# A two-block transformer step on one core: small operations of the linear-attention solve go to ScalarE, its end is written in a new order, and key products stand among the pair products

## The reference, cut to what matters

```python
def _rwkv7_step(S, inp):
    r, w, k, v, a, b = inp
    sa = jnp.einsum('bhvk,bhk->bhv', S, a)
    S = S * w[:, :, None, :] + sa[..., None] * b[:, :, None, :] + v[..., None] * k[:, :, None, :]
    y = jnp.einsum('bhvk,bhk->bhv', S, r)
    return S, y

    S0 = jnp.zeros((B, H, N, N), f32)
    _, y = lax.scan(_rwkv7_step, S0, seq)
    mean = jnp.mean(y, axis=-1, keepdims=True)
    var = jnp.mean(jnp.square(y - mean), axis=-1, keepdims=True)
    yn = ((y - mean) * lax.rsqrt(var + LNX_EPS)).reshape(B, T, D) * lnx_w + lnx_b
    bonus = (jnp.sum(rh * kh * r_k, axis=-1, keepdims=True) * vh).reshape(B, T, D)
    out = ((yn + bonus) * g).astype(x.dtype)
    return out @ w_o
...
    x = x + rmsnorm(m, norm_g[layer, 1])
    f = conv_ffn(rmsnorm(x, norm_g[layer, 2]), ffn_w_in[layer], ...)
```

## Time and profile before

| | us |
|---|---|
| median of 3 runs | 1098.86 |
| lowest and highest of the 3 | 1093.63, 1102.5 |
| the profiled execution, its own time | 1091.18 |
| the profiled execution, its span on the core | 1089.3 |
| PE busy in the span | 1062.2 (98%) |
| DVE, ACT, POOL busy | 798.9, 604.0, 219.3 |
| the stretch that the change touches, from the second pair products to the first feed-forward tile | 122 to 219 |

### The profile page before, as it was taken

How to read it: one execution, slowest core, us unless ns; L and a number is a source line. 1 busy time by engine, 2 the same in 40 slices (tenths; PEclk the granted TensorE clock), 3 DMA queues, 4 the chain that set the end, 5 groups by cost and what they waited for, 6 DMA issues and landing times.

```text
span 1089.3 us, 18693 instructions
## 1 busy us (share of the span) xinstructions
PE 1062.2 (98%) x7143; PEld 917.0 (84%) x7143; DVE 798.9 (73%) x1103; ACT 604.0 (55%) x928; POOL 219.3 (20%) x234
## 2 busy tenths in 40 slices
PE   7999998999999999999999999999999999999997
PEld 6997797888888888789888888998777789888886
DVE  7997878778886658777788756688867776666643
ACT  6766363555564566856666554635665446555532
POOL 0125493121221011002222200571100001122200
PEclk9999999999999999999999999999999999999999
DMA  8553172646666466345667575556452555766552
GB/s 249 172 172 117 39 244 69 175 135 181 187 192 253 167 151 162 121 131 150 187 189 192 194 271 158 159 191 215 154 136 84 194 162 131 193 191 193 193 193 78
DMA packets 219747, 183.11 MB, mean 168 GB/s; under 512 B 43265, under 2 KB 197614, under 8 KB 219678
## 3 DMA queue, kind: packets, MB, share of 16 engines
q1 hardware_dynamic: 215710, 171.43, 52.4%
q0 software_dynamic: 3392, 8.66, 2.5%
q10 hardware_dynamic: 576, 2.07, 0.5%
HBM read 179.44 MB, written 2.69 MB: 167 GB/s over the span
## 4 chain that ended last, share of the span: by engine, by line
PE 80%; DVE 13%; issue 2%; DMA 2%; ACT 1%; POOL 1%; SPq 1%; DVEq 0%; POOLq 0%; ACTq 0%
PE bank L288 20%; PE bank L282 13%; PE bank L284 13%; PE bank L283 13%; PE bank L289 10%; DVE ring L417 3%; PE bank L295 2%; PE bank L1250 2%; DVE arena L1687 1%; DVE arena L1782 1%; DVE stat L1780 1%; PE bank L375 1%; PE bank L2167 1%; DMA arena<-in_kv_w_up 1%; PE bank L1365 1%
## 5 line engine op out<-in xcount | busy, mean ns | idle before, releaser
L417 DVE TENSOR_TENSOR ring<-ring,arena 128x2048 fp32r<-128x2048 f32 (+1 forms) x138 | 312.9, 2271 | 112.4 <-ACT arena L411 110.8
L282 PE MATMUL bank<-arena 128*128 128x512 f32 (+3 forms) x980 | 343.6, 351 | 3.7 <-DVE ring L417 3.0
L288 PE MATMUL bank<-arena 128*128 128x512 f32 x960 | 335.7, 396 | 0.0
L411 ACT ACTIVATE arena<-ring 128x2048 fp32r<-128x2048 f32 (+1 forms) x145 | 272.1, 1879 | 98.0 <-DMA ring<-in_ffn_w_out 42.9
L289 PE MATMUL bank<-arena,ring 128*128 128x256 f32 x960 | 267.2, 278 | 0.0
L284 PE MATMUL bank<-arena 128*128 128x512 f32 (+3 forms) x720 | 264.7, 368 | 0.0
L283 PE MATMUL bank<-ring,arena 128*128 128x512 f32 (+2 forms) x560 | 216.1, 386 | 0.0
L288 PEld LDWEIGHTS bank<-arena 128*128 128x128 f32 x960 | 180.1, 188 | 42.6
L282 PEld LDWEIGHTS bank<-arena 128*128 128x128 f32 x980 | 185.4, 189 | 29.2 <-issue 5.4
L289 PEld LDWEIGHTS bank<-arena,ring 128*128 128x128 f32 x960 | 180.6, 188 | 0.0
L284 PEld LDWEIGHTS bank<-arena 128*128 128x128 f32 x720 | 135.6, 188 | 22.2
(11 more groups left out here) (338 smaller groups left out, 1274.9 us busy)
## 6 DMA issues: line engine op xcount, KB each, us to landing
ring<-in_ffn_w_in SPq DMA_DIRECT2D x80, 512.0 KB, 5.1
ring<-in_ffn_w_out SPq DMA_DIRECT2D x44, 512.0 KB, 4.4
ring<-in_w_gate_up SPq DMA_DIRECT2D x40, 512.0 KB, 5.1
ring<-in_w_in SPq DMA_DIRECT2D x18, 1024.0 KB, 5.1
ring<-in_a_w_rkv SPq DMA_DIRECT2D x12, 1024.0 KB, 5.4
ring<-in_w_down SPq DMA_DIRECT2D x22, 512.0 KB, 3.7
ring<-in_a_w_o SPq DMA_DIRECT2D x4, 1024.0 KB, 6.8
arena<-in_ffn_w_in SPq DMA_DIRECT2D x8, 512.0 KB, 4.7
```

The costliest lines, as they stand in the source:

```text
L282: nc.tensor.matmul(dst, stationary[0], moving[0], start=start, stop=False)
L288: nc.tensor.matmul(dst[:, :], stationary[0], both_parts, start=start, stop=False)
L411: nc.scalar.activation(buf(hi_of(n), 0, w, arena12), ring[:, r, 0:w], ACT.Copy).then_inc(hi_ready, 1)
L417: on.tensor_tensor(ring12[:, r, 0:w], ring[:, r, 0:w], buf(hi_of(n), 0, w, arena12).bitcast(F32), ALU.subtract).then_inc(split_ready, 1)
```

## The change

It has these parts:

1. **Key products among pair products.** On PE `key_values(0)` stands behind bank 9 and `key_values(1)` behind bank 12 of the second pass, instead of both behind bank 15.
2. **Means of the values.** DVE sums both chunks in one reduction and no longer scales; ACT scales (`v_mean`), before its first `step_evac`. POOL's `values_centred` waits for that.
3. **Variance.** DVE keeps the reduction (`squares_summed`); ACT does the scaling (`variance`).
4. **Scaling of the outputs.** The multiplication of a bank by the root moves from one DVE operation to eight ACT operations, one for each head (`scaled`), so `gated_out` has two DVE operations left.
5. **Order on DVE.** The first sum of squares stands ahead of `state_added`; both `gated_out` of chunk 0 stand behind the last `block_added`; the last `w_o` split stands ahead of `gated_out(1, 0)`; `early_lo(0)` leaves the solve for the passage, and `early_lo(1)` goes behind the first turn there.
6. **Order on PE.** `block_inverses(1, 1)` stands ahead of `o_turn(0, 0)`; `o_turn(1, 1)` stands ahead of tile (1, 0), not (1, 1).
7. **Order on ACT.** The squares of chunk 1 stand closer together, and the second `w_o` slot's high part is split once the state products are done.
8. **POOL** waits for the low part of the first `w_o` slot before `values_centred(1)`.

Two semaphores are renamed: `means_ready` is `stats_ready` (it counts the sums too), `u_out` is `solve_out` (it counts `scaled` too, so `EARLY_OUT0` is 8).

```diff
@@ ffn_front_dve
             if f != 1:
+                early_lo(dve, f, 0 if f == 0 else 1)
+            turn_dve(dve, turn, 0, 4, hi, lo)
+            if f == 0:
                 early_lo(dve, f, 1)
-            turn_dve(dve, turn, 0, 4, hi, lo)
@@ rwkv_pe
             pe.wait_ge(tok_evac, 4)
-            for l in range(PAIR_BANKS):
-                if l >= 4:
-                    pe.wait_ge(prod_evac, PAIR_BANKS + l - 3)
-                pairs(l, key, l // 8).then_inc(prod_mm, 1)
...
-            pe.wait_ge(v_evac, 4)
-            key_values(0)
-            key_values(1)
+            for l in range(PAIR_BANKS):
+                if l >= 4:
+                    pe.wait_ge(prod_evac, PAIR_BANKS + l - 3)
+                pairs(l, key, l // 8).then_inc(prod_mm, 1)
+                if l == 9:
+                    pe.wait_ge(v_evac, 4)
+                    key_values(0)
+                elif l == 12:
+                    key_values(1)
             pe.wait_ge(z_landed, 16 * NT * NB)
             pe.wait_ge(cleared, NT * NB + 1)
             pe.wait_ge(prod_evac, 2 * PAIR_BANKS)
...
             block_inverses(1, 0)
+            block_inverses(1, 1)
             o_turn(0, 0)
-            block_inverses(1, 1)
...
                 elif (a, s) == (1, 0):
+                    o_turn(1, 1)
                     pe.wait_ge(o_split, 3)
-                elif (a, s) == (1, 1):
-                    o_turn(1, 1)
@@ rwkv_act
             def squares(a, q):
                 act.wait_ge(ymm, 2 * a + q + 1)
-                if a == 1:
-                    act.wait_ge(var_ready, 2 + q + 1)
...
+            def variance(a, q):
+                stat = slice(a * H + 8 * q, a * H + 8 * (q + 1))
+                act.wait_ge(stats_ready, 2 + 2 * a + q + 1)
+                nc.scalar.activation(y_var[:, stat], y_sq[:, stat], ACT.Copy, bias=LNX_EPS, scale=1.0 / N).then_inc(var_ready, 1)
+
+            def scaled(a, q):
+                act.wait_ge(rstd_ready, 2 + 2 * a + q + 1)
+                for h in range(8 * q, 8 * q + 8):
+                    op = nc.scalar.activation(toks(W_YC)[:, a, h * N:(h + 1) * N], bank[Y_BANK[a][q]][:, h % 8 * N:(h % 8 + 1) * N],
+                                              ACT.Copy, scale=y_rstd[:, a * H + h:a * H + h + 1])
+                op.then_inc(solve_out, 1)
...
+            act.wait_ge(stats_ready, 1)
+            nc.scalar.activation(v_mean, v_sum, ACT.Copy, scale=-1.0 / N).then_inc(stats_ready, 1)
             for b in range(4):
                 step_evac(b)
...
             squares(0, 0)
+            act.wait_ge(state_mm, 1)
+            ahead(act, FIRST["w_o"] + 1, split_act)
+            variance(0, 0)
             squares(0, 1)
+            variance(0, 1)
             ahead(act, FIRST["w_o"] + 2, split_act)
+            scaled(0, 0)
+            scaled(0, 1)
             act.wait_ge(sweep_mm, SOLVED + SWEEP_NO[1, 2])
             ahead(act, LAST["w_o"], split_act)
             solutions(1, 0)
             solutions(1, 1)
             o_evac(0, 0)
             squares(1, 0)
+            squares(1, 1)
             o_evac(0, 1)
-            squares(1, 1)
+            variance(1, 0)
+            variance(1, 1)
             early_hi(act, 0, 0)
+            scaled(1, 0)
+            scaled(1, 1)
@@ rwkv_dve, gated_out
-                dve.wait_ge(rstd_ready, 2 + 2 * a + q + 1)
-                link(dve, nc.vector.tensor_tensor(by_head(yc), by_head(bank[Y_BANK[a][q]][:, :]), spread(y_rstd[:, stat].unsqueeze(2), [P, 8, N]), ALU.mult))
+                dve.wait_ge(solve_out, 4 * a + 2 + q + 1)
@@ rwkv_dve
-            for a in range(NT):
-                value_means(a)
+            nc.vector.tensor_reduce(v_sum, by_head(buf(W_V)), AX, ALU.add).then_inc(stats_ready, 1)
...
+            squares_summed(0, 0)
             state_added(0)
             state_added(1)
-            variance(0, 0)
+            squares_summed(0, 1)
             block_added(1, 0, 1)
-            variance(0, 1)
             block_added(1, 0, 2)
             block_added(1, 1, 1)
-            gated_out(0, 0)
             block_added(1, 0, 3)
             block_added(1, 1, 2)
             block_added(1, 1, 3)
+            gated_out(0, 0)
             gated_out(0, 1)
             o_lo(0, 0)
             ahead(dve, FIRST["w_o"] + 1, split_dve)
-            variance(1, 0)
+            squares_summed(1, 0)
             o_lo(0, 1)
-            variance(1, 1)
+            squares_summed(1, 1)
             ahead(dve, FIRST["w_o"] + 2, split_dve)
+            ahead(dve, LAST["w_o"], split_dve)
             gated_out(1, 0)
-            ahead(dve, LAST["w_o"], split_dve)
             gated_out(1, 1)
             o_lo(1, 0)
-            early_lo(dve, 0, 0)
             o_lo(1, 1)
@@ rwkv_pool
-                pool.wait_ge(means_ready, a + 1)
+                pool.wait_ge(stats_ready, 2)
...
             rest_gated(0)
+            pool.wait_ge(split_ready, SPLIT_NO[FIRST["w_o"]] + 1)
             values_centred(1)
```

More of the change, by code:

```diff
@@ L1448, in rwkv_pe @@
                 if h % 8 == 0:
-                    pe.wait_ge(u_out, h // 8 + 1)
+                    pe.wait_ge(solve_out, h // 8 + 1)
                 lo, c, hv = (h % 2) * N, h // 2, slice(h * N, (h + 1) * N)
@@ L1476, in rwkv_pe @@
             block_inverses(1, 0)
+            block_inverses(1, 1)
             o_turn(0, 0)
[L1478 removed]
             for q in range(2):
[L1480 removed]
+                pe.wait_ge(solve_out, 4 + q + 1)
                 y_solved(1, q)
@@ L1638, in solutions @@
                 act.wait_ge(sweep_mm, SOLVED * a + SWEEP_NO[g, NB])
-                nc.scalar.activation(u[a][:, g * HALF:(g + 1) * HALF], bank[(0, 4)[a] + g][:, :], ACT.Copy).then_inc(u_out, 1)
+                nc.scalar.activation(u[a][:, g * HALF:(g + 1) * HALF], bank[(0, 4)[a] + g][:, :], ACT.Copy).then_inc(solve_out, 1)
             def squares(a, q):
                 act.wait_ge(ymm, 2 * a + q + 1)
-                if a == 1:
-                    act.wait_ge(var_ready, 2 + q + 1)
                 nc.scalar.activation(y_squared[q], bank[Y_BANK[a][q]][:, :], ACT.Square).then_inc(squared, 1)
+            def variance(a, q):
[8 more added lines that the diff above has]
+                op.then_inc(solve_out, 1)
             def o_evac(a, q):
@@ L1799, in at_bank, with squares_summed @@
                 return toks(W_YC)[:, a, q * HALF:(q + 1) * HALF], slice(a * H + 8 * q, a * H + 8 * (q + 1))
-            def variance(a, q):
+            def squares_summed(a, q):
                 stat = at_bank(a, q)[1]
                 dve.wait_ge(squared, 2 + 2 * a + q + 1)
-                link(dve, nc.vector.tensor_reduce(y_sq[:, stat], by_head(y_squared[q]), AX, ALU.add))
-                nc.vector.tensor_scalar(y_var[:, stat], y_sq[:, stat], 1.0 / N, LNX_EPS, ALU.mult, ALU.add).then_inc(var_ready, 1)
+                nc.vector.tensor_reduce(y_sq[:, stat], by_head(y_squared[q]), AX, ALU.add).then_inc(stats_ready, 1)
             def gated_out(a, q):
@@ L1836, in block_added @@
                 nc.vector.tensor_tensor(rhs[a][rows, cells], bank[g][rows, :], rhs[a][rows, cells], ALU.add).then_inc(sum_ready, 1)
-            def value_means(a):
-                at = slice(a * H, (a + 1) * H)
-                link(dve, nc.vector.tensor_reduce(v_sum[:, at], by_head(toks(W_V)[:, a, :]), AX, ALU.add))
-                nc.vector.tensor_scalar(v_mean[:, at], v_sum[:, at], -1.0 / N, None, ALU.mult).then_inc(means_ready, 1)
             def state_added(g):
```

11 lines of the change are left out of this document (5 added, 6 removed).

## The result

The changed kernel takes 1087.03 us (median of 4 runs, 1085.12 to 1091.76) against 1100.3 for the kernel before in the same comparison (median of 4, which include the three shown above). The ratio is 0.9893, with a 95% interval of [0.9862, 0.9923]. Repeated with more runs, it was 1087.99 (8 runs), ratio 0.9904 [0.9876, 0.9932]. The prediction had summed up 0.5 us.

A forecast was written before the change was run, and what follows sets the result against it. PE, busy in 98% of the span, was taken as the bound; time is won only where DVE, ACT or POOL end its waits last. The terms left 0.5 us at the passage; forecast 1097 us, range 1091 to 1102.

The forecast's parts named there:

- Part 2: Means of the values: the blocked 1.18 us scaling leaves DVE, POOL's first centring starts near 139.7 or later, nothing on PE.
- the signs of being right: Trace signs listed beforehand, from steps starting 1 to 2 us later than 136.47 to the clock at 0.50 near 128.
- Part 1: Keys among pair banks: +0.85 exposed copy, -0.3 filled waits, +0.6 lone banks; steps about 1.2 us later.
- the lone banks: Pair banks 12 and 15, left without a partner by the moved keys: 0.6 us taken, bounds zero and 2 x 0.5.
- Parts 3 to 5: Chunk 1's sweep: PE's 2.1 us of addition waits go, but ACT's chain leaves the w_o tiles' start unchanged (-1.5 to +1).
- ACT takes over: In chunk 1's sweep: sixteen ACT scalings end at 171.6, the solutions at 174.8, losing 2 us of the sweep's gain.
- The w_o tiles: Output tiles paced by DVE's 11.0 us chain: gate at 186.7, tile (0, 3) at 187.2 against 187.10, so zero gain.
- Part 8 and the state: POOL's wait holds DVE's first w_o low part to 154.5, ending near 156.8; the state 0.4 us late.
- The passage: Solve to feed-forward: post_scale near 191.6, chunk 0's turn wait vanishes, x_scaled ends at 204.2 against 204.70; 0.5 us left.
- The front costs nothing and ACT keeps up: Rival: state 1.2 us early, sweep saves 2.1 more; -3 us in the median, 1094 to 1096; chance 0.17.
- The front costs more than the tail returns: Rival: steps 2 us later, POOL and DVE collide at the low part; +0.3 to +2, 1099 to 1101; chance 0.22.
- The scalings bind: Rival: an ACT scaling out of PSUM takes 0.35, not 0.25 us; 1.6 before chunk 1's solutions, +1.5; chance 0.06.

The follow-up runs named there:

- the means alone: Kernel before with only one reduction of both chunks on DVE and the scaling on ACT: 1092.11 us (12 runs), ratio 0.9959.
- the POOL wait: Kernel before with one line more, POOL waiting for both means before chunk 1's read mask: 1091.44 us (12 runs), ratio 0.9948.
- second trace of before: Kernel before, unchanged, run again for another trace: 1099.4 us (10 runs), ratio 0.9998; the trace's span is 1095.2 us.
- keys and means back: Changed kernel with both key halves behind the last pair bank and the means scaled on DVE again: 1094.51 us (12 runs), ratio 0.9928.
- the passage alone: Kernel before with only o_turn(1, 1) one tile earlier and the new places of early_lo: 1095.4 us (12 runs), ratio 0.9948.
- means back: Changed kernel with the means' two reductions and two scalings on DVE again: 1088.58 us (11 runs), ratio 0.9926.
- keys alone: Kernel before with only the key products moved among the pair products: 1095.31 us (12 runs), ratio 0.9965.
- the passage back: Changed kernel with the last output turn and both early low parts placed as before: 1089.07 us (12 runs), ratio 0.9925.

## Why the prediction was wrong

**The step that failed** stands in "What bounds the kernel now", in "Nothing that I found reaches 1% (11 us) in either direction", and in Part 2, which ends "nothing on PE" and priced only "the blocked 1.18". The mechanism had been read rightly from the earlier trace rows: DVE's small scaling stands still until POOL is done. The size was taken from the one recorded execution. In most executions (66 of 79 by their times) the scaling misses the gap between two POOL operations. In the trace of such a one it is held 6.3 us, PE waits 5.4, and the clock is at half for 6.8. That is 6.5 us in the trace, 6.2 to 6.8 in the medians of the means alone and of the POOL wait.

**The clue that was passed over** stands in the sum: "Its own time lies 7.7 below the median of 1098.86". I took that for spread and moved the forecast's centre down to 1097 for it. It was the hold, and none of the three traces of the changed kernel has it. Of the signs of being right all but the first came (the steps came 2.3 us later, not 1 to 2), and the time was wrong all the same: the signs had been drawn from the recorded execution, as the sum had.

**Part 1** had its direction right. The steps came 2.3 us later, not 1.2 (bounds -0.6 and 1.9). The exposed copy was priced at 0.85 and measured 1.02; the gain of filling waits, taken as 0.3, did not show; the rest is the switching and the lone banks, priced at 0.6. The trace doesn't separate these two. In the changed kernel without part 1 the median is 2 us lower. Against the kernel before, part 1 gains, since it moves DVE and POOL apart, which no rival had.

**Parts 3 to 5** went as worked out. Sixteen scalings took 3.39 (4.0 predicted) and ended with the high part and solutions at 173.3 to 174.4 (173.5 to 174.8). "ACT takes over" held.

**The w_o tiles** came 1.2 us earlier than the "Zero" taken. The first split on DVE began at 175.03, not 175.5, and the gate was ready at 185.5, 1.2 before the 186.7 predicted, as DVE's chain took 10.5 and not 11.0 to it. It lies within the bounds given. From the end of chunk 0 on, the gain is 3.8 us (54.93 to 51.09), where the prediction's steps add up to 0.9 (0.4 late to 0.5 early); most of that difference is the sweep and the tiles, taken as zero.

**Part 8 and the state.** POOL's first L1948 at 140.73 (139.7 or later), the low part 155.15 to 157.43 (156 to 158), at 2.28 since POOL now waits for it. The state was to be 0.4 us late; chunk 0 ends 1.5 late (table, -4.3 against -5.8), as the steps had come 1.1 later than predicted.

**The passage**: `post_scale` at 190.64 and 202.96 (191.6 and 204.2 predicted), no wait at chunk 0's turn and 0.9 at chunk 1's (about 1). Relative to the recorded execution the first feed-forward tile is 2.4 us early, 0.5 predicted. Of the other 1.9, 1.2 are there already at chunk 1's `post_scale`, as much as the gate came before its forecast; the last 0.7 lies behind it and was not followed. In the second trace of before the turn's wait of 1.99 also has a low stretch of 3.4 us behind it, worth 1.6, which the recorded execution did not show. The sum had no term for it.

**The rivals.** "The front costs nothing and ACT keeps up" gave 1094 to 1096, the front did cost, and the time is lower than that still. "The front costs more than the tail returns" had its condition met, 2.3 us at the steps against the 1.7 that it names, but not its outcome, 1099 to 1101. "The scalings bind" did not come: a scaling takes 0.21. The range's low end, 1091, was built from effects of 4 us and the spread of a median; it had no term for a mechanism that the recorded execution did not contain. The whole gain of 11 to 13 us in the medians is made up of 6 to 7 us from the hold, less 2 that the interleaved keys cost, and the rest, 6.7 by the kernel with keys and means back. In the traces that rest is 5.5: 2.8 for the new end of the solve and the output, 1.1 for the passage and 1.6 for the low clock that goes with its wait. The 2.8 is a difference between traces; the parts in it (3 to 8 without the passage) were not run one by one. The medians give 1 to 2 us more than the traces, also for the passage alone (4.7 against 2.7), and where that lies stays open.

## What to carry to other kernels

When the profiled execution is several us away from the median of the same kernel, it may not be a typical one: take a second trace, or name a mechanism for the gap and price it as a rival, before the sum is made from its rows. A small DVE operation that is caught behind POOL has two prices, the rest of one POOL operation or that of all that follow back to back, and in these traces the two lie close together (1.14 us left of the first operation, or 1.33). Here one wait on POOL's queue, or the scaling moved to ACT, removed it.

## What the runs showed of the hardware

**A held DVE operation can be passed over by the next POOL operation.** In six traces a `TENSOR_SCALAR` of 16 columns met POOL's 1.9 us operation, with another ready behind it. Where 1.79, 1.81 and 1.33 us were left of the first (before's second trace, the passage alone, keys and means back), it was held through the second as well, and in the latter two its record ends only with the memset behind that (143.98 and 144.38), so it took 7.19 and 6.71. Where 1.14, 0.83 and 0.83 were left (before's first, means back, keys alone), it ran between the two. That the time left is what decides is a reading of these six and was not varied by itself. The Trainium skill, "SBUF — State Buffer", section "Who interferes with whom", lets the shared ports be locked for a whole instruction; the trace agrees for each of the two, 1.91 and 4.49. A `TENSOR_REDUCE` was not held: in the means alone L1830, which reads a bank, took its usual 0.68 at 137.82, inside POOL's L1934 (137.26 to 139.17), and in the recorded execution of before L1840, which reads SBUF, began at 134.90 inside L1907 (131.08 to 135.63) and took its usual 1.21.

**The clock answers the same wait differently.** PE idles 1.8 to 2.0 us before the fifth bank in all 14 traces. The granted clock fell to 0.50 (1.2 GHz) behind it in four of them (the recorded execution of before, two of the changed kernel, keys and means back) and stayed at 1.00 in ten. Behind 2.0 us at the turn it fell in three traces (before's second, the means alone, one POOL wait) and not in three (before's first, the keys alone, the passage back). These low stretches were 3.4 us long, and 6.8 with the 4.7 to 5.7 us of idling at the first sweep, where the clock fell while PE still stood. Each trace also ends in a low stretch, of 2.7 to 5.7 us. Why the same wait has one or the other answer stays open.
